# Leaving out the matrix products that nobody reads, in a one-core kernel of two chained blocks

## The reference

```python
def first_block(x, ...):
    h = rmsnorm(x, norm1_g)
    z_glu, z_rx, z_rg, z_ga, z_gb = split(h @ w_in + b_in)
    u = silu(layernorm(causal_depthwise_conv(z_glu..., 31 taps)))      # y_a = u @ conv_w_out
    hb = rg_lru(causal_depthwise_conv(z_rx, 4 taps), ...)              # y_b = (hb * gelu(z_rg)) @ lru_w_out
    x = x + (sigmoid(z_ga) * y_a + sigmoid(z_gb) * y_b) @ w_mix_out
    h = rmsnorm(x, norm2_g)
    x = x + (silu(h @ ffn_w1) * (h @ ffn_w3)) @ ffn_w2
    return rmsnorm(x, norm_f_g)

def second_block(x, c, ...):                     # sh, sc, gt: nine rows made from c
    h = rmsnorm(x, g_pre[0]) * (1 + sc1) + sh1
    x = x + 0.5 * gt1 * rmsnorm(swiglu(h, ...), g_post[0])
    h = rmsnorm(x, g_pre[1]) * (1 + sc2) + sh2
    x = x + gt2 * rmsnorm(token_mixer(h, ...), g_post[1])   # gated linear attention and softmax attention
    h = rmsnorm(x, g_pre[2]) * (1 + sc3) + sh3
    return x + 0.5 * gt3 * rmsnorm(swiglu(h, ...), g_post[2])
```

## The kernel before, in words

| place | products before the broadcast | between two broadcasts | behind |
|---|---|---|---|
| the beginning | 14 before the sums, 4 behind them | - | 10 |
| norm behind mix | 5 | - | 10 |
| behind block 1 | 12 | 0 | 6 |
| `two_roots(7)`, behind ffn(2) | 0 | 2 | 8 |
| `two_roots(9)`, behind wout | 0 | 2 | 8 |

## Time and profile before

### The profile page before, as it was taken

One profiled execution on the slowest core, in us unless ns is written; L12 is line 12 of the kernel. 1 busy time (PEld: TensorE's weight loads), 2 busy tenths in 40 slices (PEclk: granted clock), 3 DMA queues, 4 the chain that ended last, 5 costly groups with the idle time before them and its releaser, 6 DMA issues.

```text
span 2313.0 us, 33192 instructions
## 1 busy us (share of the span) xinstructions
PE 2273.6 (98%) x10598; PEld 1871.7 (81%) x10598; DVE 1009.8 (44%) x1667; ACT 899.1 (39%) x1624; POOL 1032.0 (45%) x788
## 2 busy tenths in 40 slices
PE   8999999999999999999999999999899999999997
PEld 7888888888888888888888778888677787888886
DVE  6899886436513314110014325555765556110112
ACT  4334663332222333332333354444665453332332
POOL 3455553454444443444445343333222453444444
PEclk9999999999999999999999999999999999999998
DMA  4333444338737532333332223334311432333331
GB/s 153 95 96 102 144 114 150 96 110 287 277 113 231 169 96 65 104 95 96 98 97 87 78 80 110 111 110 135 103 51 55 151 92 71 97 96 100 93 98 60
DMA packets 129482, 263.95 MB, mean 114 GB/s; under 512 B 14256, under 2 KB 14384, under 8 KB 128624
## 3 DMA queue, kind: packets, MB, share of 16 engines
q1 hardware_dynamic: 119520, 236.51, 33.4%
q10 hardware_dynamic: 9872, 26.25, 3.0%
HBM read 250.02 MB, written 12.58 MB: 114 GB/s over the span
## 4 chain that ended last, share of the span: by engine, by line
PE 74%; issue 14%; POOL 6%; DVE 4%; ACT 1%; DMA 0%; POOLq 0%; ACTq 0%; DVEq 0%
PE bank L995 23%; PE bank L997 23%; PE bank L996 23%; POOL wlo L414 6%; PE bank L1346 1%; PE bank L1412 1%; PE bank L1390 1%; DVE bank L1661 1%; PE bank L1159 1%; PE bank L1072 0%; PE bank L1135 0%; PE bank L1143 0%; DMA cols<-d_cols 0%; PE bank L1119 0%; DVE bank L1732 0%
## 5 line engine op out<-in xcount | busy, mean ns | idle before, releaser
L414 POOL TENSOR_TENSOR wlo<-raw,whi 128x512 fp32r<-128x512 f32 x750 | 990.5, 1327 | 1219.2 <-ACT whi L485 1218.5
L995 PE MATMUL bank<-a_hi,whi 128*128 128x512 f32 x1928 | 762.6, 396 | 9.3 <-DVE a_lo L1472 5.4
L997 PE MATMUL bank<-a_lo,whi 128*128 128x512 f32 x1928 | 751.1, 390 | 0.0
L996 PE MATMUL bank<-a_hi,wlo 128*128 128x512 f32 x1928 | 750.5, 389 | 0.0
L485 ACT ACTIVATE whi<-raw 128x512 fp32r<-128x512 f32 x750 | 469.1, 628 | 687.0 <-PE bank L997 616.5
L995 PEld LDWEIGHTS bank<-a_hi,whi 128*128 128x128 f32 x1928 | 362.0, 188 | 93.5 <-issue 10.3
L997 PEld LDWEIGHTS bank<-a_lo,whi 128*128 128x128 f32 x1928 | 361.9, 188 | 76.7
L996 PEld LDWEIGHTS bank<-a_hi,wlo 128*128 128x128 f32 x1928 | 362.1, 188 | 75.5 <-issue 1.4
L995 PE MATMUL bank<-b_hi,whi 128*128 128x512 f32 x852 | 335.0, 393 | 0.6 <-DVE b_lo L1799 0.3
L997 PE MATMUL bank<-b_lo,whi 128*128 128x512 f32 x852 | 331.6, 389 | 0.0
L996 PE MATMUL bank<-b_hi,wlo 128*128 128x512 f32 x852 | 331.5, 389 | 0.0
(11 more groups left out here) (273 smaller groups left out, 1823.2 us busy)
## 6 DMA issues: line engine op xcount, KB each, us to landing
raw<-d_stream SPq DMA_DIRECT2D x750, 256.0 KB, 2.6
G<-d_ada SPq DMA_DIRECT2D x72, 512.0 KB, 4.6
spill_rv<-tmp ACTq DMA_DIRECT2D x32, 256.0 KB, 2.0
G<-spill_rv ACTq DMA_DIRECT2D x8, 1024.0 KB, 8.0
G<-d_x ACTq DMA_DIRECT2D x4, 512.0 KB, 5.5
spill_ga<-sq ACTq DMA_DIRECT2D x8, 256.0 KB, 3.4
G<-spill_ga ACTq DMA_DIRECT2D x1, 2048.0 KB, 8.4
G<-d_x ACTq DMA_DIRECT2D x1, 2048.0 KB, 13.7
```

The lines of the kernel that those rows point to most:

```text
L414: pool.tensor_tensor(wlo[:, s % SRING, :], raw[:, s % RING, :], whi[:, s % SRING, :].bitcast(F32), ALU.subtract).then_inc(lo_done, 1)
L995: pe.matmul(out_ps, w_hi, hi[:, k, :], start=first and q == 0, stop=False)
L996: pe.matmul(out_ps, w_lo, hi[:, k, :], start=False, stop=False)
L997: mm = pe.matmul(out_ps, w_hi, lo[:, k, :], start=False, stop=last and q == len(ks) - 1)
```

## The change

All calls of `keep_warm`, the function itself, and the parameter `warm` of `broadcast` are removed. Nothing else changes: the same sums, broadcasts, stages and waits remain in the same order.

```diff
--- before.py
+++ after.py
@@ -1107,9 +1107,7 @@
 
 
                 broadcast(n, src=ROOT1)
-                keep_warm(2, 3)
                 broadcast(n + 1, src=ROOT2, dst=bank[6])
-                keep_warm(8, 3)
 
             def sum_pairs():
 
@@ -1128,16 +1126,9 @@
                                    start=(k == 0 and tt == 0), stop=(k == KD - 1 and tt == 3), skip_group_check=True)
                 mm.then_inc(sq_summed, 1)
 
-            def keep_warm(n, where=7):
-
-
-                for _ in range(n):
-                    pe.matmul(bank[where][:, 0:P], ones[:, :], ones[:, :], start=True, stop=True)
-
-            def broadcast(n, src=small[:, 1, 0:4], dst=BCAST, warm=0):
-
-
-                keep_warm(warm)
+            def broadcast(n, src=small[:, 1, 0:4], dst=BCAST):
+
+
                 pe.wait_ge(st_ready, n)
                 for j in range(4):
                     mm = pe.matmul(dst[:, j * P:(j + 1) * P], src[:, j:j + 1].to_broadcast([P, P]), ident,
@@ -1186,10 +1177,8 @@
                     sum_up(norm)
 
             pe.wait_ge(const_ready, 1)
-            keep_warm(14)
             sum_pairs()
-            broadcast(1, warm=4)
-            keep_warm(10)
+            broadcast(1)
             wide_stage("win", OPA, opa, FILL_A["h1"], 9)
 
             def lru_gates(half):
@@ -1233,12 +1222,10 @@
             for m in range(KD):
                 tile8("mix", 0, m, OPB, opb, FILL_B["mix"], m == 0)
             sum_up(NORM["n2"])
-            broadcast(4, warm=5)
-            keep_warm(10)
+            broadcast(4)
             ffn(1, NORM["nf"], True, FILL_A["hf1"])
-            broadcast(5, src=small[:, 5, 0:4], warm=12)
+            broadcast(5, src=small[:, 5, 0:4])
             broadcast(6, src=small[:, 4, 0:4], dst=bank[6])
-            keep_warm(6)
             ffn(2, NORM["post1"], False, FILL_A["hf2"])
             two_roots(7)
```

## The result

Over 8 runs each the kernel before took 2317.39 us and the changed one 2324.56 us (medians): ratio 1.0032, 95% interval 1.0023 to 1.0041. In a second measurement, against 18 runs of the kernel before, it was 2324.24 against 2316.81, ratio 1.0035 (1.0022 to 1.0049). So leaving the 81 products out costs about 7.3 us. One of the 8 executions of the changed kernel took 9088 us with a mean granted clock of 0.546; the median of 2324.56 counts it (2324.23 without), the ratio leaves it out, and the profile shown is of another execution, with a span of 2322.5 us.

A forecast was written before the change was run, and what follows sets the result against it. TensorE, busy 98% of the span, was taken to bound the kernel. Terms 2.1 + 1.65 + 2.25 + 1.4 + 1.4 gave +8.8 us, so 2323.6 from the profiled execution or 2326.0 from the median; forecast 2325.0, range 2318.5 to 2330.

The forecast's parts named there:

- The case named: Half clock outlasts the restart of the wide products at all five places; 2325.0 us, own range 2321 to 2331, chance 0.68.
- The price of half clock: For 512-wide products on TensorE, each microsecond at half clock loses 0.47 us of progress, from steps of 0.426 against 0.226 us.
- 4.5 us past the first wide product at each place: At the beginning and four turns, half clock lasts 4.5 us from the first wide product, bounds 0 and 6.1.
- The beginning, +2.1: At the kernel's start, nothing gained in the queue and 2.1 us lost to the clock.
- no gain (0 to 0.1): At the beginning, the 14 unread products cost nothing, nor do the 4 before and 10 behind the broadcast; gain 0 to 0.1 us.
- The norm behind mix, +1.65: At mix's norm, the stage starts 0.45 us sooner but the clock costs 2.1 us; net +1.65 us.
- Behind block 1, +2.25: Behind the first block, broadcast 0.40 us sooner but 0.54 lost at half clock, plus 2.1 from the clock; +2.25 us.
- the 2.1 us of the clock: Behind block 1, as at each place, 4.5 us at half clock past the restart cost 2.1 us, between 0 and 2.9.
- rival A: Where a turn has two broadcasts, their 16 passes may lift the clock; only beginning and mix's norm pay; +3.9, about 2321; chance 0.18.
- The second block's turns, +1.4 each: At the second block's two turns, stage start unmoved, 2.1 us lost to the clock less 0.7 recovered; +1.4 us each.
- The recovery of 0.7 us: In the second block's turns, VectorE's slack of 0.23 to 0.25 us a group lets late TensorE recover three times, 0.7 us.
- Rival B: At all five places each broadcast brings the clock back before the stage; only queue places count, 2316.3 us; chance 0.10.

The follow-up runs named there:

- `behind`: The kernel before with only the 42 unread products behind each place's last broadcast kept, the 39 others left out; 2318.6 us, ratio 1.0010.
- `ahead`: The kernel before with only the unread products ahead of and between the broadcasts kept, the 42 behind the last broadcasts left out; 2322.81 us, ratio 1.0026.
- `narrow`: The kernel before with all 81 unread products in place, each streaming one column instead of 128; 2331.49 us, ratio 1.0067.
- `turns_out`: The kernel before with the 53 unread products at the four turns left out, the 28 at the beginning kept; 2323.06 us, ratio 1.0030.
- `more`: The kernel before with more unread products wherever TensorE has nothing to do, such as ahead of first sums and between broadcasts; 2318.12 us, ratio 1.0000.

## Why the prediction was right, and where its steps were not

**The total.** Forecast 2325.0, measured 2324.56; 7.2 us slower where 7.9 over the shown median was forecast. The case named was the one that happened, at four of its five places. But the hit is partly luck. The sum of 8.8 us is made of five terms that measured 6.0 in the profiles: three were too large by 2.0, 0.7 and 0.6, two too small by 0.35 and 0.1. And 3.7 us in the profiles (about 1.3 in the medians: their 7.3 less the 6.0 of the five places), from the layer norm and va, no step had.

**What is lost comes by the clock, not by the place in the queue.** Shown, by `behind` and `ahead` (the 42 products behind the last broadcasts alone, or the 39 others alone: 1.8 and 6.0 us over before), and by `narrow` (the same places in the queue, without bringing the clock back: 14.7 us).

**The price of half clock,** 0.47 us per us: right. In the changed kernel the first group of turn 1 took 5.12 us, 0.427 a product, against 0.226. The Trainium skill, "TensorE: Matmul & The Clock Gate", section "Terms", has 0.50; the trace comes near. At the beginning, from the first wide product to the layer norm's sums, it took 333.34 us against a mean of 330.65, so 5.7 us at half clock cost 2.7, which is 0.47 again.

**4.5 us past the first wide product at each place:** mis-sized; the mean over the places was 3.2. In the three profiles it was 5.7, 3.6 and 3.3 at the beginning, 3.2, 3.9 and 3.8 behind mix, nothing behind block 1, and on average 5.0 and 3.0 in the second block's turns. Of the four rows that the 4.5 came from, three count from the first pass of unread work or of the broadcast, and va's 4.4, called the nearest, holds a microsecond at full clock; its half clock was 3.3 to 3.4 us.

**The beginning, +2.1:** mis-sized. The profiles say +1.4, whole-kernel time no difference to be measured. The step compared with a profile in which the 10 products behind the broadcast cost nothing; in the second profile of before they ran at half clock and cost 1.4, and of the changed kernel's three profiles only the first lost 5.7 us to half clock. The step "no gain (0 to 0.1)" failed, since the cover it named depends on where the clock stands.

**The norm behind mix, +1.65:** +2.0. The stage's start moved as said in the profiles where the unread passes had ended late (9.64 and 9.65 us behind the first sum, 9.26 without them), but one of the three of before had 8.73: the mean gain is 0.07, not 0.45. The stage behind it lost 2.06 (from its first wide product to block 1's first sum 384.66 against 382.60). At 0.47 the 3.6 us of half clock are 1.7 of that; the other 0.4 is not explained.

**Behind block 1, +2.25:** the step that failed; +0.3. The broadcast ran slower, as said (12.26 us from sum to stage against a mean of 11.97); that it starts sooner holds only against the first profile of before (7.72 us behind the first sum against 8.13, but 7.72 and 7.73 in the other two). What failed is the 2.1 us of the clock: it was back 0.7 to 0.9 us ahead of the first wide product in all three profiles, at the end of the two broadcasts, and from there on to turn 1's sums it took 359.4 us in both kernels. That is what rival A said would happen, at this one place. I had put it aside because the clock had not risen in 5.3 us of unread passes from 892.65; but what counts is the state at the first wide product, and the 16 passes of broadcast begin 4.5 us ahead of it. That these 16 passes are enough is not shown: in `narrow` the same 16, from 906.62, left the clock at half, and it came back only at 918.5. There it had fallen 5.2 us ahead of the broadcasts, and here 3.0 to 3.2.

**The second block's turns, +1.4 each:** +1.5 (3.1 less the 1.6 of va) and +0.8. The start of the stages did not move (13.60 and 13.6 us behind the first sums against 13.6, with 14.20 once before), so the slower second broadcast was covered, as said. The recovery of 0.7 us is seen: 5.0 us at half clock cost 2.3 by the price and 1.7 were found (3.33 behind the first wide product of turn 1, less the 1.6 of va); 3.0 us cost 1.4 and 0.77 were found.

**Rival B,** clock back everywhere, 2316: refuted by the products 0.43 us apart behind four of the five starts.

**Open.** Why va's half clock is 6.8 us long in the five profiles of kernels whose turn 1 has no full-width unread products (the changed one three times, `turns_out`, `narrow`), and 3.4 or none in the eight others. Nothing in va differs. It may be that where the clock rose in one turn sets where it falls and rises in the next places, but that is not shown: no run varied it alone. With it, 1.6 us of the change's cost in the profiles are located, not explained; the same holds for the layer norm, whose steps of 1.6 us came in kernels that are alike up to there.

## What to carry to other kernels

Work that nobody reads is not free time to be collected: 28.2 us of it here held the path up by up to 1.4 us at a place, in some executions, and with it the kernel is 7.3 us faster than without. Before removing or adding such work, look at the granted clock at the first real product behind it, in more than one profile of the same kernel, because in some executions the same filler costs what it buys in others. What the runs favour is full-width filler that runs up to that product and ends there (`behind`); filler ahead of a gap was worth little (`ahead`), filler that runs past the operand delays it (`more`, +2.6 us), and one-column filler delays it without bringing the clock back (`narrow`).

## What the runs showed of the hardware that was not expected

A pass of one column took 0.21 us at half clock, as long as one of 128 columns there (4.27 and 4.08 us for 20), and kept the stage waiting (`narrow`). Two executions of the same kernel differ by lumps of 1.6 us, one length of 3.4 us at half clock, at places where TensorE never stood idle for more than 0.9 us (layer norm: 143.08 and 144.66, and 146.24 in `turns_out`, a kernel alike up to there). The 16 passes of two broadcasts in a row ended with the clock back in four profiles (the changed kernel's three and `turns_out`) and still at half in `narrow`. And the profile's clock column shows nothing before the first recorded change: 1.00 at 24 to 29 us with products 0.43 us apart.
